# A two-layer decoder trunk on one core: where each engine takes its batches of expert pairs is read from a table, in place of step lengths and a common lag

## The chip, the cores and the metric

The kernel runs on one core of a Trainium2 chip, in one launch. The metric is the device time of that launch in microseconds (us), the median over runs. The core has five engines that run their own instruction streams and meet on semaphores: TensorE (PE in the profile), VectorE (DVE), ScalarE (ACT), GpSimd (POOL) and SyncE (SP), and 16 DMA engines that all of them feed.

## The reference, cut to what matters

```python
for l in range(DEPTH):                       # DEPTH = 2, x is (1, 256, 1024) f32
    h = _rmsnorm(x, norm_mix_g[l])
    z = h @ w_in[l]                          # split into q, k, v, gates, conv and pool inputs
    ...                                      # sparse attention, conv branch, pooling branch
    x = x + jnp.concatenate([o_nsa, o_conv, o_pool], axis=-1) @ w_out[l]
    x = x + _cross_attention(_rmsnorm(x, norm_xa_g[l]), _rmsnorm(mem, norm_mem_g[l]), xa_wq[l], xa_wkv[l], xa_wo[l])
    x = x + _peer(_rmsnorm(x, norm_ffn_g[l]), peer_wq[l], peer_subkeys[l], peer_u[l], peer_v[l])
return _rmsnorm(x, final_g)

def _peer(h, wq, sub_keys, u, v):            # per token: 8 heads x 16 experts = 128 pairs
    ...                                      # top 16 of each key half, top 16 of their 256 sums
    act = jax.nn.gelu(jnp.einsum('cd,chkd->chk', hc, u[ic]))      # ic: 128 expert numbers a token
    return jnp.einsum('chk,chkd->cd', gc * act, v[ic])
```

Each of the 256 tokens picks 128 of 16384 experts in each layer. An expert is one row of `u` and one of `v`, 1024 numbers each, so a token's pair is 8 KB that must be gathered from memory.

## The kernel before

The 256 tokens are two tiles of 128, and with two layers there are four pieces of dense work (everything but the experts' sums) and four of expert work. The program is five stages, written by one function `stage(dense, experts, ...)`. The first stage does the dense work of layer 0, tile 0. Stages 1, 2 and 3 each do the dense work of the next tile and, woven into it, the expert work of the tile before. The last stage has only expert work and what is left of the ranking of its experts. In the profiled execution the stages 1, 2, 3 and last begin at 217.4, 633.5, 1035.8 and 1432.3 us.

**Expert work.** A stage has 128 pairs, `k` = 0 to 127. GpSimd issues one gather a pair (`gather`, L521): 128 rows of 8 KB, one a token, into one of 10 slots of `uv_rows` (`ROWS`). Two pairs are a batch, so a stage has 64 batches (`NB`). For each pair of a batch VectorE forms the dot product of the gathered `u` rows with the tokens (L566), ScalarE takes the gelu and scales a 128x64 diagonal with it (L1029, L1036), and TensorE multiplies the `v` rows with that diagonal and adds them up in PSUM (L1307, four matmuls a pair); its last matmul frees the slot (`slots_free`), and GpSimd may gather the pair that stands 10 further on. The first 10 gathers of the next stage are issued in this manner at the end of a stage, as soon as a quarter of its experts is ranked (`gates0`).

**Dense work.** Its steps stand in a list (`PLAN`; stage 1 has `MEM_PLAN`, with the keys and values of layer 1's memory besides; the last stage `LAST_PLAN`). An engine that has part in a step runs it when the list comes to it; `zk2`, for instance, is a product on TensorE and a copy on ScalarE, `rope` is VectorE alone. The weights are loaded by SyncE in units of 1 MB, each as soon as the unit that held its place has been used; stages 1 and 3 have 7 places, stage 2 has 3 (the two first blocks go to places that stage 3 still uses). The product of four units with a rows' operand is L1361 or L1337.

**The order of the two.** Each engine's program is one sequence. The helper `run` goes through the list, and behind each step it puts as many batches as the table `turns` has for that engine and step:

```python
for step_name in ["start"] + plan:
    if step_name in steps:
        steps[step_name]()
    n = turns.get(name, {}).get(step_name, 0)
    if n:
        batch_run(b, b + n)
        b += n
```

`turns` is worked out by `spread`: each step has a length (`LENGTH`), the batches are dealt out in proportion to the lengths passed, VectorE and ScalarE get the same numbers (ScalarE one batch later at the start), and TensorE stands one batch behind them (`LAG`). Stages 2 and 3 have one table. In the last stage 21 batches are dealt out over the ranking, and the rest follows behind it. The ranking of a quarter of the experts is seven steps on VectorE: `rank`, `rank_more`, `rank_pairs`, `rank_pairs_more`, `gates`, `look_up`, `look_up_more`; of these ScalarE has part in `gates` alone.

Of the kernel before, what the change touches and what calls it, by code (L numbers as in the profile page):

```python
# [41 lines left out]
NB = PAIRS // B  # L42
# [26 lines left out]
for _name, _w in (("causal", S), ("cadd", TILES * NC), ("cvalid", TILES * NC), ("cur", 4 * P), ("prev", 4 * NC),  # L69
# [95 lines left out]
LAST_PLAN = ["rank1", "rank_more1", "rank_pairs1", "rank_pairs_more1", "gates1", "look_up1", "look_up_more1",  # L165
             "rank2", "rank_more2", "rank_pairs2", "rank_pairs_more2", "gates2", "look_up2", "look_up_more2",
             "rank3", "rank_more3", "rank_pairs3", "rank_pairs_more3", "gates3", "look_up3", "look_up_more3",
             "first_out"]


LENGTH = {"mix_norm": 4, "ab": 4, "zq": 4, "zk1": 4, "zk2": 4, "conv_in": 0, "conv": 2, "rope": 3, "branch_gates": 0,
          "sel_exps": 0, "win_exps": 0, "sel_values": 4, "win_values": 4, "turn_kv": 5, "rank": 3, "rank_more": 2, "rank_pairs": 3, "rank_pairs_more": 3, "look_up": 3, "look_up_more": 3,
          "gates": 2, "first_out": 2, "cmp_in": 6, "cmp_hidden": 6,
          "cmp_hidden_turn": 2, "cmp_kv": 2, "cmp_scores": 4, "sel_scores": 4, "sel_more": 3, "cmp_probs": 3, "cmp_out": 3,
          "sel_turn": 4, "win_scores": 4, "win_more": 3, "sel_out": 2, "conv_norm": 4, "win_turn": 4, "conv_act": 3, 
          "win_out": 2, "small_branches": 3, "mix_turn": 2, "wo": 9, "xa_norm": 7, "xq": 8, "xa_scores": 6,
          "xa_turn": 4, "xa_out": 4, "xo": 9, "ffn_norm": 8, "pq": 8, "sub_scores": 2, "mem_kv": 8}
LAG = 1
AT_START = 1


def spread(plan, within):

    lengths = [LENGTH[name if name in LENGTH else name.rstrip("0123456789")] for name in plan]
    vector, tensor, done, passed = {"start": AT_START}, {}, 0, 0
    for name, length in zip(plan, lengths):
        passed += length
        due = within * passed // sum(lengths)
        vector[name] = due - done
        tensor[name] = max(due - LAG, 0) - max(done - LAG, 0)  # L190
        done = due
    scalar = {**vector, "start": 0, plan[0]: vector[plan[0]] + AT_START}
    tensor[plan[0]] += AT_START
    return {"vector": vector, "scalar": scalar, "tensor": tensor}


TURNS = spread(PLAN, NB - 2)
MEM_TURNS = spread(MEM_PLAN, NB - 2)
LAST_TURNS = spread(LAST_PLAN, 21)


TURN_PARTS = [6.25]
# [26 lines left out]
def build_program(nc, a):  # L229
    with ExitStack() as ctx:  # L230
        def sb(name, shape, dt=F32):
            return ctx.enter_context(nc.sbuf_tensor(name, shape, dt))
# [23 lines left out]
        conv = sb("conv", [P, 2, P])  # L256
# [14 lines left out]
        gates = sb("gates", [P, 24])  # L271
# [20 lines left out]
        cmp_in = area2[:, 0:1024].rearrange("p (k c n) -> p k c n", k=2, c=16)  # L292
# [35 lines left out]
        def stage(dense, experts, mem_layer=None, first=False, last=False):  # L328


            plan = LAST_PLAN if last else FIRST_PLAN if first else PLAN if mem_layer is None else MEM_PLAN
            turns = {} if first else LAST_TURNS if last else TURNS if mem_layer is None else MEM_TURNS
            if dense is not None:
                layer, tile = dense // TILES, dense % TILES
            own_half = dense is not None and tile == 0
# [98 lines left out]
            def run(eng, name, steps, batch_run):  # L434

                b = 0
                for step_name in ["start"] + plan:
                    if step_name in steps:
                        steps[step_name]()
                    n = turns.get(name, {}).get(step_name, 0)  # L440
                    if n:
                        batch_run(b, b + n)
                        b += n
                if experts is not None:
                    batch_run(b, NB)


            with nc.Block(no_gpsimd_drain=not last) as block:
# [109 lines left out]
                def _(dve):  # L558
# [420 lines left out]
                    for i in range(4):  # L979
                        steps[f"gates{i}"] = lambda i=i: expert_gates(i)  # L980
                        signal = "routed" if i else "first_routed"
                        for part, more in enumerate(("", "_more")):
# [6 lines left out]
                            if first and i == 0:  # L989
                                steps[f"rank{more}0_later"] = lambda p=part: rank_half(range(2, 4), p)  # L990
                                steps[f"rank_pairs{more}0_later"] = lambda p=part: rank_pairs(range(1, 2), p)
                                steps[f"look_up{more}0_later"] = lambda p=part: look_up(range(1, 2), "first_routed", p)
                    run(dve, "vector", steps, batch_run)
                    if experts is not None:
                        experts_end()
# [14 lines left out]
                def _(act):  # L1010
# [271 lines left out]
                    if first:  # L1282
                        steps["pq0"] = lambda: queries("PQ0", 0, 2)
                        steps["pq0_later"] = lambda: queries("PQL", 2, 2)
                        steps["sub_scores0"] = lambda: sub_scores("PK0", 0, 2)
                        steps["sub_scores0_later"] = lambda: sub_scores("PKL", 2, 2)
                    run(act, "scalar", steps, batch_run)
                    if last:
                        for c in range(2):
# [7 lines left out]
                def _(pe):  # L1297
# [378 lines left out]
                    if first:  # L1676
                        steps["pq0"] = lambda: cols_product("PQ0", "pq0", [0])
                        steps["pq0_later"] = lambda: cols_product("PQL", "pq0", [1])
                        steps["sub_scores0"] = lambda: sub_scores("PK0", 0, 2, 1)
                        steps["sub_scores0_later"] = lambda: sub_scores("PKL", 2, 2, 2)  # L1680
                    run(pe, "tensor", steps, batch_run)


            nc.gpsimd.sem_clear(range(stage_sems[0], stage_sems[-1] + 1))
            nc.all_engine_barrier(sem_only=True)

        stage(0, None, mem_layer=0, first=True)
        stage(1, 0, mem_layer=1)
        for s in range(1, STAGES - 1):
            stage(s + 1, s)  # L1690
# [117 lines left out]
```

## Time and profile before

| | us |
|---|---|
| median of 3 runs | 1760.89 (1759.98 to 1761.31) |
| the profiled execution's own time | 1762.63 |
| its span | 1760.8 |
| PE, DVE, ACT, POOL busy | 1338.8, 1094.5, 515.2, 663.1 |
| moved by DMA | 689.00 MB, of it 536.90 MB by GpSimd's gathers |

The busy times are those of the whole span. GB/s of a stretch is what all DMA engines moved in it, gathers and weights together. A gather is 128 x 8 KB, 1.05 MB.

### The profile page before, as it was taken

The numbers are of one execution on the slowest core, as the hardware profiler recorded it, in microseconds if no ns is written. First come the engines' busy times: TensorE is split into PE (matmuls) and PEld (weight loads), VectorE is DVE, ScalarE is ACT, GpSimd is POOL, SyncE is SP. The second block draws the span as 40 slices with busy tenths as digits, with TensorE's granted clock in tenths as the row PEclk, the third lists the DMA queues.
The fourth block names the chain that finished last, engine by engine and source line by source line (L and its number), as shares of the span: only waits on it lengthen the run. The fifth ranks groups of instructions, "written<-read, shape, count | busy, mean of one in ns | idle before, by whom it ended". The sixth has DMA issues, their size and how long they took to land. (4 is left out here: it accounts for less than half of the span.)

```text
span 1760.8 us, 22766 instructions
## 1 busy us (share of the span) xinstructions
PE 1338.8 (76%) x8310; PEld 686.1 (39%) x8310; DVE 1094.5 (62%) x2746; ACT 515.2 (29%) x1295; POOL 663.1 (38%) x1028
## 2 busy tenths in 40 slices
PE   8999886679999857667888766767888865565655
PEld 5856842245564523222354433233354531111111
DVE  5510588984333849779434757798444868964444
ACT  3411232262312222226332222225332323221112
POOL 0000234344333424435434434344433545565451
PEclk9999988799999978878989888778999977887778
DMA  9755599999999999999999999999999999999996
GB/s 387 293 169 182 209 421 421 414 394 422 411 421 421 420 410 405 421 396 414 422 421 422 421 421 420 422 386 421 421 421 421 421 418 400 407 420 422 421 421 272
DMA packets 95728, 689.00 MB, mean 391 GB/s; under 512 B 11008, under 2 KB 11136, under 8 KB 12288
## 3 DMA queue, kind: packets, MB, share of 16 engines
q0 software_dynamic: 73728, 536.90, 74.0%
q1 hardware_dynamic: 21888, 150.64, 21.3%
q8 instruction: 66, 1.08, 0.2%
q14 instruction: 46, 0.38, 0.1%
HBM read 685.40 MB, written 2.10 MB: 390 GB/s over the span
## 5 line engine op out<-in xcount | busy, mean ns | idle before, releaser
L521 POOL DMA_INDIRECT uv_rows<-uv_in,idx x512 | 504.0, 984 | 1055.5 <-PE acc_pe L1307 817.5
L1307 PE MATMUL acc_pe<-uv_rows,diag 64*64 64x512 f32 x4096 | 616.5, 731 | 322.7 <-ACT diag L1036 307.9
L566 DVE CUSTOM_DVE_ANT_0 uv_rows<-uv_rows,h_ps 128x1024 f32<-128x1024 f32 x512 | 606.7, 1218 | 232.4 <-DMA uv_rows<-uv_in,idx 220.6
L1307 PEld LDWEIGHTS acc_pe<-uv_rows,diag 64*64 64x64 f32 x4096 | 154.5, 153 | 693.1 <-ACT diag L1036 481.8
L1029 ACT ACTIVATE gelu_b<-act_b,h_scale 128x2 f32<-128x2 f32 x255 | 75.0, 294 | 744.0 <-DVE act_b L566 739.1
L1337 PEld LDWEIGHTS bank<-h_t,w_own 128*128 128x128 f32 x1504 | 171.0, 193 | 18.0 <-issue 18.0
L1361 PE MATMUL bank<-w_own,h_t 128*128 128x512 f32 x384 | 176.0, 612 | 2.3 <-ACTq L1077 2.2
L1337 PE MATMUL bank<-h_t,w_own 128*128 128x128 f32 x1504 | 175.1, 278 | 0.0
L515 POOL TENSOR_TENSOR diag<-ident_st,gate 128x64 f32<-128x64 f32 x512 | 159.0, 311 | 9.6
L1036 ACT ACTIVATE diag<-diag,gelu_b 128x64 f32<-128x64 f32 x510 | 149.6, 340 | 8.3
L1361 PEld LDWEIGHTS bank<-w_own,h_t 128*128 128x128 f32 x384 | 73.2, 196 | 107.8 <-issue 103.7
L828 DVE TENSOR_TENSOR xs<-xs,bank 128x512 f32<-128x512 f32 x16 | 11.0, 688 | 160.1 <-PE bank L1361 160.1
L1074 ACT ACTIVATE area<-bank 128x512 f32<-128x512 f32 (+2 forms) x77 | 43.2, 561 | 226.4 <-PE bank L1337 130.0
L680 DVE SCALAR_TENSOR_TENSOR conv<-hc,smalls,conv 128x128 f32<-128x128 f32 x240 | 68.3, 355 | 0.4
L1332 PE MATMUL bank<-ident,area 128*128 128x128 f32 x216 | 36.0, 319 | 30.6 <-ACT area L1049 20.6
L1029 ACT ACT_TABLE_LOAD x40 | 51.3, 1283 | 1.8
L1332 PEld LDWEIGHTS bank<-ident,area 128*128 128x128 f32 x216 | 28.7, 163 | 50.8 <-issue 23.1
L566 DVE DVE_READ_ACCUMULATOR2_ANT act_b<- 128x1 f32 x512 | 42.1, 82 | 0.0
L864 DVE MAX8 half_v<-area 128x8 f32<-128x128 f32 x128 | 28.0, 279 | 19.2 <-ACTq L1077 18.9
L598 DVE TENSOR_TENSOR h_t<-bank,smalls 128x512 f32<-128x512 f32 x24 | 15.7, 688 | 36.6 <-PE bank L1332 27.7
L867 DVE FIND_INDEX8 half_i<-half_v,area 128x8 uint32<-128x128 f32 x128 | 34.2, 285 | 0.0
L1337 PE MATMUL bank<-h_t,uv_rows 128*128 128x128 f32 x288 | 32.9, 275 | 1.0 <-DVE h_t L598 1.0
(208 smaller groups left out, 1170.5 us busy)
## 6 DMA issues: line engine op xcount, KB each, us to landing
w_own<-blocks_in SPq DMA_DIRECT2D x112, 1024.0 KB, 10.5
uv_rows<-blocks_in SPq DMA_DIRECT2D x24, 1024.0 KB, 10.4
uv_rows<-uv_in,idx POOLq DMA_INDIRECT x512, 15.4
xs<-x_in SPq DMA_DIRECT2D x2, 512.0 KB, 13.5
uv_rows<-mem_in SPq DMA_DIRECT2D x1, 1024.0 KB, 13.8
mem_gained<-uv_rows SPq DMA_DIRECT2D x1, 1024.0 KB, 14.1
area<-mem_gained SPq DMA_DIRECT2D x1, 1024.0 KB, 8.9
smalls<-smalls_in SPq DMA_DIRECT2D x1, 816.5 KB, 13.5
```

The lines of the kernel that those rows point to most:

```text
L515: nc.gpsimd.tensor_tensor(diag[:, slot_of(k, earlier), :], ident_st[:, :], gate[:, k:k + 1].to_broadcast([P, HT]), ALU.mult).then_inc(sems ...
L521: nc.gpsimd.indirect_dma_start(uv_rows[:, slot_of(k, earlier), :, :].rearrange("p a n -> p (a n)"), None, a["uv"], bass.IndirectOffsetOnAx ...
L566: v.tensor_tensor_reduce(u_row, u_row, h_ps[:, :], 1.0, 0.0, ALU.mult, ALU.add, act_b[:, k // B % AHEAD, k % B:k % B + 1]).then_inc(sems[" ...
L680: ins = v.scalar_tensor_tensor(out=conv[:, g, :], in0=hc[:, g, k:k + P], scalar=small("cw", g * CONV_W + k, 1), in1=conv[:, g, :], op0=ALU ...
L867: step.mark(v.max_index(where[:, g, lo], top[:, g, lo], values(g)))
L1029: s.activation(gelu_b[:, b % AHEAD, :], act_b[:, b % AHEAD, :], ACT.Gelu_apprx_tanh, scale=h_scale[:, 0:1]).then_inc(sems["gelu_done"], 1)
L1036: s.activation(diag[:, slot_of(k), :], diag[:, slot_of(k), :], ACT.Copy, scale=gelu_b[:, b % AHEAD, k % B:k % B + 1]).then_inc(sems["diag_ ...
L1074: drain(s.activation(out, src, func, **kw), job)
L1307: mm = pe.matmul(acc_pe[c * HT:(c + 1) * HT, r * BLK:(r + 1) * BLK], diag[tok, slot_of(k), :], uv_rows[tok, slot_of(k), 1, c * BLK:(c + 1) ...
L1332: mm = pe.transpose(out[:, i * P:(i + 1) * P], src, ident[:, :])
L1337: mm = pe.matmul(out, lhs, rhs, start=(i == 0), stop=(i == len(pairs) - 1))
L1361: mm = pe.matmul(out[:, :], lhs[:, c, :], w[:, i, :], start=(c == 0), stop=(c == KC - 1))
```

## The change

`LENGTH`, `LAG`, `AT_START` and `spread` go, and with them the three tables that it made. In their place stands a table that is written out: for each of the stages 1, 2, 3 and last (`None`), for each step, how many batches VectorE, ScalarE and TensorE run behind it. The steps, their order on each engine, the order of the batches, the gathers' and weights' order and all waits stay as they were; in the last stage and the others every batch now stands in the table (64 a stage).

```diff
-LENGTH = {"mix_norm": 4, "ab": 4, "zq": 4, "zk1": 4, "zk2": 4, "conv_in": 0, "conv": 2, "rope": 3, "branch_gates": 0,
...
-          "xa_turn": 4, "xa_out": 4, "xo": 9, "ffn_norm": 8, "pq": 8, "sub_scores": 2, "mem_kv": 8}
-LAG = 1
-AT_START = 1
-
-
-def spread(plan, within):
-
-    lengths = [LENGTH[name if name in LENGTH else name.rstrip("0123456789")] for name in plan]
-    vector, tensor, done, passed = {"start": AT_START}, {}, 0, 0
-    for name, length in zip(plan, lengths):
-        passed += length
-        due = within * passed // sum(lengths)
-        vector[name] = due - done
-        tensor[name] = max(due - LAG, 0) - max(done - LAG, 0)
-        done = due
-    scalar = {**vector, "start": 0, plan[0]: vector[plan[0]] + AT_START}
-    tensor[plan[0]] += AT_START
-    return {"vector": vector, "scalar": scalar, "tensor": tensor}
-
-
-TURNS = spread(PLAN, NB - 2)
-MEM_TURNS = spread(MEM_PLAN, NB - 2)
-LAST_TURNS = spread(LAST_PLAN, 21)
+BATCHES = {
...
+        "xa_turn": (0, 1, 1), "xa_out": (2, 2, 2), "xo0": (3, 1, 0), "ffn_norm": (2, 3, 3), "pq0": (1, 1, 2),
...
+    None: {
...
+        "first_out": (38, 41, 40),
+    },
+}
+ENGINES = ("vector", "scalar", "tensor")
...
-            turns = {} if first else LAST_TURNS if last else TURNS if mem_layer is None else MEM_TURNS
+            batches = {} if first else BATCHES[dense]
...
-                    n = turns.get(name, {}).get(step_name, 0)
+                    n = batches[step_name][ENGINES.index(name)] if step_name in batches else 0
```

What this does to the sequences is shown at three places. One line's number in the new kernel is 39 higher than the same line's in the old one.

**TensorE at the start of stage 2.** The rows run from the transposes of the normed tokens through the product `zq` (the first L1361) and `ab` (L1337) to `zk1`. Eight matmuls of `acc_pe` are one batch. Before:

```order
L1332 MATMUL bank<-ident,area 128x128 x8
L1307 MATMUL acc_pe<-uv_rows,diag 64x512 x8
L1361 MATMUL bank<-w_own,h_t 128x512 x8
L1307 MATMUL acc_pe<-uv_rows,diag 64x512 x8
L1337 MATMUL bank<-h_t,w_own 128x128 x32
L1307 MATMUL acc_pe<-uv_rows,diag 64x512 x24
L1361 MATMUL bank<-w_own,h_t 128x512 x8
```

And with the change:

```order
L1371 MATMUL bank<-ident,area 128x128 x8
L1400 MATMUL bank<-w_own,h_t 128x512 x8
L1346 MATMUL acc_pe<-uv_rows,diag 64x512 x32
L1376 MATMUL bank<-h_t,w_own 128x128 x32
L1346 MATMUL acc_pe<-uv_rows,diag 64x512 x16
L1400 MATMUL bank<-w_own,h_t 128x512 x8
```

The batch ahead of `zq` is gone from there, and four stand between `zq` and `ab` where one stood.

**TensorE in stage 3, from `zq` to the transposes of q, k and v.** The three L1361 of before are `zq`, `zk1` and `zk2`. Before:

```order
L1361 MATMUL bank<-w_own,h_t 128x512 x8
L1307 MATMUL acc_pe<-uv_rows,diag 64x512 x8
L1337 MATMUL bank<-h_t,w_own 128x128 x32
L1307 MATMUL acc_pe<-uv_rows,diag 64x512 x24
L1361 MATMUL bank<-w_own,h_t 128x512 x8
L1307 MATMUL acc_pe<-uv_rows,diag 64x512 x40
L1361 MATMUL bank<-w_own,h_t 128x512 x8
L1307 MATMUL acc_pe<-uv_rows,diag 64x512 x16
L1332 MATMUL bank<-ident,area 128x128 x8
```

And with the change:

```order
L1400 MATMUL bank<-w_own,h_t 128x512 x8
L1376 MATMUL bank<-h_t,w_own 128x128 x32
L1346 MATMUL acc_pe<-uv_rows,diag 64x512 x24
L1400 MATMUL bank<-w_own,h_t 128x512 x8
L1346 MATMUL acc_pe<-uv_rows,diag 64x512 x40
L1400 MATMUL bank<-w_own,h_t 128x512 x8
L1346 MATMUL acc_pe<-uv_rows,diag 64x512 x8
L1371 MATMUL bank<-ident,area 128x128 x8
```

With the batch ahead of `zq`, which is gone too, 8 batches now stand ahead of `zk2` where 10 stood, and 9 ahead of the transposes where 12 stood. On VectorE `rope` stands between the two: behind 10 batches where it stood behind 11.

**VectorE in the last stage, from the end of the first ranked quarter.** L936 ends `look_up_more1`; MAX, MAX_INDEX and MATCH_REPLACE are `rank2`, the next MAX and MAX_INDEX `rank_more2`; a pair is two rows of L566, a batch four. Before:

```order
L936 TENSOR_TENSOR idx<-area 128x32
L566 ISA uv_rows,act_b<-uv_rows,h_ps 128x1024
L566 ISA act_b 128x1
L566 ISA uv_rows,act_b<-uv_rows,h_ps 128x1024
L566 ISA act_b 128x1
L864 MAX half_v<-area 128x8 x4
L867 MAX_INDEX half_i<-half_v,area 128x8 x4
L871 MATCH_REPLACE area<-half_v,area 128x128 x4
L566 ISA uv_rows,act_b<-uv_rows,h_ps 128x1024
L566 ISA act_b 128x1
```

And with the change:

```order
L975 TENSOR_TENSOR idx<-area 128x32
L903 MAX half_v<-area 128x8 x4
L906 MAX_INDEX half_i<-half_v,area 128x8 x4
L910 MATCH_REPLACE area<-half_v,area 128x128 x4
L903 MAX half_v<-area 128x8 x4
L906 MAX_INDEX half_i<-half_v,area 128x8 x4
L605 ISA uv_rows,act_b<-uv_rows,h_ps 128x1024
L605 ISA act_b 128x1
L605 ISA uv_rows,act_b<-uv_rows,h_ps 128x1024
L605 ISA act_b 128x1
```

The batches behind `look_up_more1` and behind `rank2` are moved to later places. Over the stage, the batches that stand behind VectorE's steps are these (steps from `start`; a dot where there is none): before, one behind `start` and one behind each of the 22 steps but for `rank_more1`; now none behind `start`, then 1 1 . 1 1 2 . for the first quarter, . 1 3 . 1 . 1 for the second, 2 . 2 1 2 6 1 for the third, and the last 38 behind `first_out`.

**Elsewhere, in numbers of batches ahead of a step.** TensorE comes to `zk2` behind 6, 8 and 8 batches in stages 1, 2 and 3, where it had 8, 10 and 10; in stage 1 to `sel_values0` behind 21, where it had 23; in stage 2 to `xo0` behind 43, where it had 45, and then runs none behind `xo0` and `xo1`, where it ran two behind each, and three behind the transposes of `ffn_norm`. In stage 3 it runs 44 ahead of `xa_out` and no more until behind those transposes. VectorE comes to `xo0` in stage 2 behind 44 batches, where it had 46; in both kernels TensorE runs 17 batches ahead of the compression product of stage 2.

## Rows read from the trace of the kernel before

**Rows 1.** the page, part 2: GB/s in 40 slices of 44 us

```profile
GB/s 387 293 169 182 209 421 421 414 394 422 411 421 421 420 410 405 421 396 414 422 421 422 421 421 420 422 386 421 421 421 421 421 418 400 407 420 422 421 421 272
```

**Rows 2.** busy time by stretch; last columns granted clock, DMA share, GB/s

```profile
core 0: us, PE busy (x) PEld busy (x) DVE busy (x) ACT busy (x) POOL busy (x), PEclk, DMA share, GB/s
217.00:320.00 103.00, 71.95 (x396) 32.00 (x400) 89.74 (x286) 28.63 (x66) 37.09 (x56) 0.82 1.01 421
320.00:400.00 80.00, 61.41 (x487) 31.04 (x487) 72.82 (x166) 42.78 (x108) 35.95 (x56) 0.89 1.00 403
...
610.00:690.00 80.00, 59.20 (x396) 32.47 (x388) 52.83 (x159) 22.40 (x51) 32.11 (x51) 0.87 1.00 406
...
740.00:780.00 40.00, 22.53 (x175) 7.81 (x179) 29.55 (x75) 6.16 (x21) 13.39 (x20) 0.70 0.99 391
...
1130.00:1170.00 40.00, 26.70 (x224) 10.46 (x223) 36.40 (x95) 13.34 (x37) 17.35 (x27) 0.74 0.97 382
...
1430.00:1550.00 120.00, 64.81 (x356) 16.23 (x360) 103.26 (x293) 31.72 (x80) 56.75 (x86) 0.76 1.00 407
1550.00:1740.00 190.00, 112.97 (x644) 27.16 (x640) 96.76 (x160) 35.28 (x120) 96.89 (x152) 0.77 1.01 421
```

**Rows 3.** who waited for whom over the whole span: total, times, longest

```profile
POOL uv_rows L521 <- PE acc_pe L1307: 817.5, 276, 18.8
...
DVE uv_rows L566 <- DMA uv_rows<-uv_in,idx: 220.6, 144, 3.8
...
DVE area L697 <- ACTq L1077: 18.2, 3, 8.0
```

**Rows 4.** timeline of stage 3: start, length, engine, line; idle time before it

```profile
1110.34 8.12 PE L1361 MATMUL bank<-w_own,h_t 128*128 128x512 f32 x16
...
1118.57 0.60 ACT L1074 ACTIVATE area<-bank 128x512 f32<-128x512 f32 x1 [6.39 <-PE bank L1361]
...
1119.24 0.27 DVE L697 TENSOR_TENSOR area<-area,cos_t 128x112 f32<-128x112 f32 x1 [8.02 <-ACTq L1077]
```

**Rows 5.** gathers' issue at the start of stage 2

```profile
662.03 0.97 POOL L521 DMA_INDIRECT uv_rows<-uv_in,idx  x1 [8.22 <-PE acc_pe L1307]
...
671.71 0.98 POOL L521 DMA_INDIRECT uv_rows<-uv_in,idx  x1 [6.93 <-PE acc_pe L1307]
```

**Rows 6.** busy time by stretch, right behind the issue of 671.71

```profile
672.00:680.00 8.00, 8.00 (x44) 3.12 (x37) 6.94 (x19) 4.06 (x7) 7.12 (x11) 1.00 0.94 320
```

**Rows 7.** PE at the compression step of stage 2

```profile
754.78 2.80 PE L1471 MATMUL bank<-w_own,area 128*32 128x256 f32 x48 [0.82 <-DVE area L723]
765.24 1.94 PE L1471 MATMUL bank<-w_own,area 128*32 128x256 f32 x16 [7.67 <-DMA w_own<-blocks_in]
```

**Rows 8.** GpSimd at the compression step of stage 2

```profile
769.40 0.97 POOL L521 DMA_INDIRECT uv_rows<-uv_in,idx  x1 [13.82 <-PE acc_pe L1307]
```

**Rows 9.** the chain that ended last, start of the last stage and 21st batch

```profile
1434.38 1.22 DVE uv_rows L566
...
1439.92 1.22 DVE uv_rows L566
...
1444.29 0.69 DVE area L903
...
1447.75 1.22 DVE uv_rows L566
...
1451.94 1.13 DVE uv_rows L566
...
1457.36 1.13 DVE uv_rows L566
...
1462.16 1.22 DVE uv_rows L566
...
1467.87 1.13 DVE uv_rows L566
...
1539.20 1.21 DVE uv_rows L566
```

More of the change, by code:

```diff
@@ L168 @@
              "first_out"]
-LENGTH = {"mix_norm": 4, "ab": 4, "zq": 4, "zk1": 4, "zk2": 4, "conv_in": 0, "conv": 2, "rope": 3, "branch_gates": 0,
[L172 to L176, printed above, removed]
-          "xa_turn": 4, "xa_out": 4, "xo": 9, "ffn_norm": 8, "pq": 8, "sub_scores": 2, "mem_kv": 8}
@@ L197 @@
-TURNS = spread(PLAN, NB - 2)
-MEM_TURNS = spread(MEM_PLAN, NB - 2)
-LAST_TURNS = spread(LAST_PLAN, 21)
+BATCHES = {
[7 rows of a table added]
+        "sel_scores": (1, 0, 0), "sel_exps": (0, 0, 1), "cmp_probs": (0, 0, 1), "conv4": (1, 1, 0),
+        "conv5": (0, 0, 1), "cmp_out": (1, 0, 0), "win_scores": (0, 2, 0), "win_more": (1, 0, 0),
+        "win_exps": (0, 2, 0), "conv6": (1, 0, 0), "conv7": (0, 0, 1), "sel_values0": (1, 1, 2),
+        "sel_values1": (0, 1, 0), "sel_out": (1, 0, 1), "conv_norm": (0, 0, 1), "win_turn": (1, 0, 0),
+        "conv_act": (1, 1, 1), "win_values1": (0, 0, 1), "win_out": (2, 1, 0), "small_branches": (0, 2, 0),
+        "mix_turn": (0, 0, 2), "wo0": (2, 2, 0), "wo1": (0, 0, 1), "xa_norm": (1, 1, 0), "xq0": (4, 3, 3),
+        "xq1": (0, 0, 1), "xa_scores": (1, 1, 1), "xa_turn": (3, 2, 2), "xa_out": (0, 1, 1), "xo0": (0, 3, 0),
[4 rows of a table added]
+    },
[7 rows of a table added]
+        "cmp_hidden_turn": (1, 0, 0), "cmp_kv": (0, 0, 1), "conv2": (0, 0, 1), "cmp_scores": (0, 1, 0),
+        "sel_scores": (1, 1, 3), "sel_exps": (1, 1, 0), "cmp_probs": (2, 0, 0), "conv4": (1, 0, 0),
+        "conv5": (0, 1, 1), "cmp_out": (0, 1, 1), "sel_turn": (0, 1, 0), "win_scores": (1, 0, 0),
+        "win_more": (1, 0, 0), "win_exps": (1, 0, 0), "conv7": (0, 1, 1), "sel_values0": (2, 2, 2),
+        "sel_values1": (0, 1, 1), "sel_out": (2, 3, 1), "conv_norm": (0, 0, 1), "win_turn": (2, 1, 0),
+        "conv_act": (1, 0, 1), "win_out": (0, 0, 1), "small_branches": (0, 1, 1), "mix_turn": (3, 4, 1),
+        "wo1": (1, 0, 4), "xa_norm": (0, 1, 0), "xq0": (2, 0, 0), "xq1": (0, 2, 2), "xa_scores": (1, 1, 0),
+        "xa_turn": (0, 1, 1), "xa_out": (2, 2, 2), "xo0": (3, 1, 0), "ffn_norm": (2, 3, 3), "pq0": (1, 1, 2),
[3 rows of a table added]
+    },
[8 rows of a table added]
+        "cmp_kv": (1, 0, 1), "conv2": (0, 0, 1), "conv3": (1, 2, 0), "cmp_scores": (0, 0, 1), "sel_scores": (2, 0, 1),
+        "sel_exps": (0, 1, 0), "cmp_probs": (0, 1, 0), "conv4": (0, 1, 0), "cmp_out": (3, 1, 1),
+        "sel_turn": (1, 0, 1), "win_scores": (0, 1, 0), "win_exps": (0, 1, 1), "conv6": (0, 1, 0), "conv7": (0, 0, 1),
[3 rows of a table added]
+        "xq1": (2, 1, 0), "xa_turn": (2, 2, 3), "xa_out": (2, 1, 0), "xo1": (1, 2, 0), "ffn_norm": (0, 2, 3),
[3 rows of a table added]
+    },
[6 rows of a table added]
+        "first_out": (38, 41, 40),
+    },
+}
```

40 rows, old and new, of the table BATCHES are left out of this document.

## Prediction

> **What bounds the kernel now.** I read the GB/s line first, since an engine's busy share over the span says little about a kernel that moves 689 MB. From the sixth slice on nearly every slice stands at 420 to 422 GB/s [rows 1], although no engine is full there: the DMA engines are the bound, and 421 GB/s is their rate. The first 200 us are slower, but the change does not touch that stage. The waits say the same: GpSimd waits 817.5 us in all for TensorE to free a slot, and VectorE 220.6 us for gathers to land [rows 3]. Neither is a fault, since a full queue looks like this from both ends.
>
> So the bytes set the time, and the order of the batches can only give or take time in which the DMA engines had too little in their queue. How much is that? I cut the span into stretches where the rate holds and where it sags. Against 421 (217 to 320 us and 1550 to 1740 us), the sagging stretches lose (421 - rate) / 421 of their length [rows 2]:
>
> - 320 to 400 us (stage 1): 403, 3.4 us
> - 610 to 690 us (end of stage 1, start of stage 2): 406, 2.85 us
> - 740 to 780 us (stage 2): 391, 2.85 us
> - 1130 to 1170 us (stage 3): 382, 3.7 us
> - 1430 to 1550 us (last stage): 407, 4.0 us
>
> Together 16.8 us, about 1% of the time. That is the most that this change can win. Behind 1740 us there is only the tail of the last batches, in an order that stays.
>
> The rate is a gather's price: 1.05 MB at 421 GB/s is 2.49 us, so a batch is worth 4.98 us of DMA time, and 10 slots are at most 25 us of cover.
>
> **The change part by part.** No instruction is added or removed; batches move against steps. A freed slot refills the queue, so what counts is when TensorE frees a batch, and whether VectorE gets through its dense steps early enough. I take the five stretches in turn.
>
> *Start of stage 2.* Now TensorE runs one batch, the product `zq`, another, `ab`, then three. GpSimd could issue two gathers at 662.03 us and the next at 671.71 [rows 5], and from 672 to 680 us, before the late ones can deliver, the rate is 320 GB/s [rows 6], 1.9 us lost in 8. In the new order `zq` runs first and four batches follow it. They wait for nothing but VectorE, which does two of them ahead of `rank1` and two right behind `rank_more1`. The four should be free by about 665 us where two were: two batches more, 10 us of queue. I take 2.5 us back; between 0 and 2.85.
>
> *Stage 3, 1130 to 1170 us.* Here VectorE is the slow one: 36.4 of 40 us busy [rows 2]. Just ahead of it VectorE stands still for 8.02 us at `rope`, until ScalarE has copied the product `zk2`, which ran from 1110.34 for 8.12 us on TensorE [rows 4]. TensorE could not start it earlier, because 10 batches stood ahead of it, the tenth of which VectorE finishes only just before. With the change 8 stand there; VectorE has still `look_up2`, `look_up_more2` and two batches to do, by the last stage's rows 2.4 + 3.3 + 2 x 2.37 = 10.4 us [rows 9], which covers 8.12 us. What is left is the wait for ScalarE, which does the same two batches before its copy, some 1.6 us. VectorE wins 6.4 us, time for 2.7 batches, or 13 us of DMA. That is more than the 3.7 us lost: I take 3.7, between 0 and 3.7. The price is that TensorE frees its first batch only behind `ab`, two products of some 8 us later. The cover is the unlanded part of the 10 gathers issued at the stage's end and the units that `zq` and `ab` set free; it should just do.
>
> The same wait is in stages 1 and 2; all three are 18.2 us [rows 3], so 10.2 us for these two. The new tables put `zk2` behind 6 and 8 batches there where 8 and 10 stood.
>
> *Stage 2, 740 to 780 us.* Beside VectorE's lag there is a wait of its own: with three places the fourth unit of the compression weights is loaded only when the first is used, TensorE stands 7.67 us for it [rows 7], and GpSimd gets no slot for 13.82 us [rows 8]. Before and after, 17 batches stand ahead of that product, so the wait stays. VectorE's part goes. I take 2.0 us; between 0 and 2.85.
>
> *Stage 1, 320 to 400 us.* VectorE is 72.8 of 80 us busy [rows 2]. It gains by its shorter wait at `rope`, but TensorE now comes to `sel_values0` with 21 batches done, not 23, and so frees two of them later. I take 2.4 us; between 0 and 3.4.
>
> *Last stage.* Here the change should cost. VectorE has no pause between 1434 and 1541 us but at `gates`, and the rate is what it leaves. From the starts of its dots [rows 9] a batch takes 2.37 us and the steps, as distances less a batch: `rank` 3.2, `rank_more` and `rank_pairs` together 5.5, `rank_pairs_more` 1.8, `gates` 3.05 (it waits for ScalarE), `look_up` 2.4, `look_up_more` 3.3, 19.3 us a quarter. A batch is late by its end minus 4.98 us for each batch before it, and the queue's loss is the greatest lateness less a constant. Before, the 21st batch ends at 1539.20 + 2.37, 107.2 us behind the first dot: late by 107.2 - 20 x 4.98 = 7.6 us. The loss measured is 4.0, so the constant is 3.6. With the change the 15th batch comes behind two quarters (the second's `gates` waits less, 18.4 us), 8.6 us of the third and 15 batches: 46.3 + 35.5 = 81.8 us, late by 81.8 - 14 x 4.98 = 12.1. The 8th, behind 28 us of steps, is late by 46.9 - 34.9 = 12.0. Loss 12.1 - 3.6 = 8.5 us, 4.5 more than now. The six batches behind `look_up3` come too late to mend it. The end of stage 3 may shift what has landed by then, by a gather or so: 2 to 6 us.
>
> *New dry spells.* In stage 2 TensorE now has no batch from `xo0` through `xo1` to the transposes of `ffn_norm`, two products of 8.12 us and some 7 us, 23 us. Four units (10 us) and up to 8 gathers are in the queue. At 6 gathers it is 25 us, and nothing is lost. Stage 3 has a like stretch with more units. I take 0.6 us; between 0 and 8.
>
> **Sum.** 2.5 + 3.7 + 2.0 + 2.4 = 10.6 us back, 4.5 + 0.6 = 5.1 us lost, 5.5 us net. From the profiled execution's 1762.63 us (its span is 1760.8, with 1.8 around it) that is 1757.1; the median of the runs is 1.74 lower, 1760.89, so 1755.4.
>
> **The rivals.** *All of it comes back, also in the last stage.* If fewer gathers have landed when the last stage begins, VectorE's lateness has more cover: three gathers fewer are 7.5 us, more than the 4.5 lost there. With the other stretches at their bounds (12.8 us) the time is about 1748. For it: the new tables differ for stages 2 and 3, where one served both. Against it: stage 3's end looks as late as before.
>
> *The gaps only move.* A queue that is refilled earlier in one place is emptier in the next, and the bytes are the same: 1761. For it: 1550 to 1740 us and 217 to 320 us show that a full queue stays full whatever the engines do [rows 2], and the places where TensorE stands behind in the new tables lie right behind those where it gained. The Trainium skill, in "DMA: Bandwidth & Descriptors", section "Issuing engines are not separate DMA queues", says that transfers issued by SyncE and GpSimd run on the same 16 engines and interleave. By that alone, weights loaded earlier take their time from gathers, and only an empty queue is worth anything; the sum would be 0 where the queue still holds a unit or a gather in the sagging stretches. The rows of this case put a price on a thin queue all the same: 320 GB/s at a DMA share of 0.94 [rows 6].
>
> *Slower: TensorE's stretch without a batch in stages 2 and 3.* If only two gathers are unlanded when `xo0` begins, cover is 5 + 10 us against 23: 8 us dry in stage 2, some 6 in stage 3 behind its `xa_turn`. With the last stage's 4.5 and 10.6 us back, 8 us net lost: 1769. It decides as soon as fewer than four gathers are in flight there. VectorE has done 44 batches and TensorE 43, which bounds them between 0 and 8.
>
> **How the numbers follow.** The forecast, 2 to 9 us faster, 0.45; all comes back, 0.16; gaps only move, within 3 us, 0.23; slower, 0.16. Half of a slower or a better case lies beyond 1766 and 1746, so the range 1745 to 1766 leaves some 0.2 out; it also holds the bounds of each term taken singly. The likeliest case's own range is 1752 to 1759. A measurement tells 0.2%, 3.5 us, from no change. Faster by more than that takes most of the first case (0.40) and the second: 0.56. Within it: the rest of the first, and the third: 0.28. Slower: 0.16.
>
> **What would show it.** Right: 421 GB/s from 672 to 680 us and through stage 3's compression step; a wait at `rope` below 3 us in each of three stages; the last stage's first 120 us below 400 GB/s, with a loss near 8.5 us. Wrong: a last stage at 407 or better, sags in the places where TensorE's batches were taken out (`xo0`, `xo1`, `wo0`, `wo1`), or the wait at `rope` unchanged.

## The result, and the profile after

The new tables make the kernel slower: median 1787.5 us (1779.7 to 1787.8, 4 runs) against 1761.1 us (1760.0 to 1764.1) in the same session, a ratio of 1.0136 (95% interval 1.0106 to 1.0167). The profiled execution took 1787.51 us, with a span of 1785.7 against 1760.8. The prediction was 1755.4, range 1745 to 1766. Two executions further down were far slower than the others of their kernel (1819.01 us of e4_new1's ten, 3182.55 us of m3_wo_xo's four): the medians count them, the ratios leave them out.

Where do the 24.9 us of span lie? The stages begin with the transposes of L1684 (L1645 before). In the profile after:

```profile
634.49 0.87 PE L1684 MATMUL h_ps<-ident,h_t 128*128 128x128 f32 x3 [4.73 <-PEq L1724]
1048.07 1.35 PE L1684 MATMUL h_ps<-ident,h_t 128*128 128x128 f32 x7 [3.20 <-PEq L1724]
1452.35 0.87 PE L1684 MATMUL h_ps<-ident,h_t 128*128 128x128 f32 x3 [4.29 <-PEq L1724]
```

Stage 1 starts at 217.2 us, where it started at 217.4. By these starts stage 1 is 1.1 us longer (417.3 for 416.1), stage 2 is 11.3 longer (413.6 for 402.3), stage 3 7.8 (404.3 for 396.5), the last 4.9 (333.4 for 328.5). The page's line of GB/s, in slices of 44.6 us, shows where stages 2 and 3 lose most, slice 18 (341) and slice 28 (346):

```profile
GB/s 387 301 166 179 223 420 421 402 394 418 406 421 421 420 421 420 422 341 420 402 401 384 421 421 405 421 421 346 412 421 400 421 420 359 422 422 421 422 421 269
```

Cut into stretches, as [rows 2] were (the last column is GB/s):

```profile
310.00:410.00 100.00, 78.38 (x528) 38.65 (x529) 82.13 (x193) 43.68 (x113) 42.93 (x66) 0.86 0.99 399
620.00:700.00 80.00, 53.86 (x328) 27.99 (x327) 56.57 (x174) 20.65 (x46) 28.13 (x43) 0.81 1.01 421
750.00:790.00 40.00, 24.33 (x180) 11.53 (x180) 28.24 (x73) 12.62 (x34) 10.59 (x16) 0.68 0.86 333
860.00:960.00 100.00, 83.70 (x560) 49.87 (x558) 37.94 (x68) 27.35 (x63) 35.57 (x56) 0.98 0.98 389
1060.00:1090.00 30.00, 30.00 (x152) 16.30 (x156) 28.07 (x87) 6.99 (x15) 8.01 (x12) 0.91 0.99 397
1130.00:1180.00 50.00, 30.52 (x219) 10.28 (x222) 44.59 (x114) 17.54 (x45) 22.64 (x36) 0.81 1.01 421
1200.00:1230.00 30.00, 16.09 (x105) 7.39 (x107) 26.25 (x56) 14.75 (x41) 8.36 (x13) 0.77 0.85 336
1350.00:1370.00 20.00, 16.51 (x107) 9.55 (x106) 9.05 (x16) 5.68 (x11) 7.65 (x12) 0.91 0.94 372
1452.00:1572.00 120.00, 62.38 (x376) 16.87 (x376) 101.34 (x288) 31.11 (x81) 60.50 (x92) 0.76 0.99 398
1572.00:1750.00 178.00, 97.59 (x572) 23.44 (x576) 91.30 (x152) 33.02 (x110) 89.35 (x140) 0.76 1.01 421
```

Counted as in the prediction, (421 - rate) / 421 of each length, two stretches won: the start of stage 2 (620 to 700 us) loses nothing where 2.85 us were lost, and stage 3 from 1130 to 1180 nothing where 3.7 were. Five lost: 750 to 790 us 8.4 (2.85 before), 860 to 960 us 7.6 (0 before), 1060 to 1090 us 1.7 (0), 1200 to 1230 us 6.1 (0), 1350 to 1370 us 2.3 (0). The last stage's first 120 us lose 6.6 (4.0 before), stage 1 5.2 (3.4). The difference of the nine is 21 of the 24.9 us; the rest is not placed.

Only SyncE (weights) and GpSimd (gathers) issue transfers while the stages run. Each of the five has its mark in GpSimd's issue of gathers, a long wait for TensorE to free a slot:

```profile
773.51 1.08 POOL L560 DMA_INDIRECT uv_rows<-uv_in,idx  x1 [27.87 <-PE acc_pe L1346]
...
942.40 0.97 POOL L560 DMA_INDIRECT uv_rows<-uv_in,idx  x1 [18.85 <-PE acc_pe L1346]
...
1078.28 0.97 POOL L560 DMA_INDIRECT uv_rows<-uv_in,idx  x1 [32.16 <-PE acc_pe L1346]
...
1214.61 0.97 POOL L560 DMA_INDIRECT uv_rows<-uv_in,idx  x1 [15.44 <-PE acc_pe L1346]
...
1359.77 0.98 POOL L560 DMA_INDIRECT uv_rows<-uv_in,idx  x1 [20.77 <-PE acc_pe L1346]
```

The first is the compression step of stage 2, where 13.82 us stood in [rows 8]. Three more long waits stand ahead of the one at 942 us:

```profile
870.99 0.97 POOL L560 DMA_INDIRECT uv_rows<-uv_in,idx  x1 [15.93 <-PE acc_pe L1346]
...
897.61 0.97 POOL L560 DMA_INDIRECT uv_rows<-uv_in,idx  x1 [15.14 <-PE acc_pe L1346]
...
912.58 0.97 POOL L560 DMA_INDIRECT uv_rows<-uv_in,idx  x1 [9.31 <-PE acc_pe L1346]
```

The kernel before had one of 12.88 us in the same place, which cost nothing:

```profile
923.26 0.97 POOL L521 DMA_INDIRECT uv_rows<-uv_in,idx  x1 [12.88 <-PE acc_pe L1307]
```

A long wait need not be dear. The one at the start of stage 2, after the change, stands in a stretch that loses nothing:

```profile
659.40 0.97 POOL L560 DMA_INDIRECT uv_rows<-uv_in,idx  x1 [26.16 <-PE acc_pe L1346]
```

The whole sum of these waits hardly moved, and the longest did (the first row below; 817.5 us and 18.8 in [rows 3]). So a total of waits says nothing here; the longest ones show where to look, but not the price. VectorE's wait at `rope` went as forecast:

```profile
POOL uv_rows L560 <- PE acc_pe L1346: 838.8, 246, 32.2
...
DVE uv_rows L605 <- DMA uv_rows<-uv_in,idx: 314.2, 207, 4.8
...
DVE area L736 <- ACTq L1116: 3.4, 3, 1.5
```

The wait at 1214 us has another engine behind it. In the profile after, TensorE waits 12.16 us for ScalarE's diagonal, and ScalarE stands in the exponentials (L1188) until VectorE has scored the second half of the heads:

```profile
1202.49 0.49 ACT L1188 ACTIVATE area<-area,st 128x256 f32<-128x256 f32 x1
...
1207.88 0.51 ACT L1188 ACTIVATE area<-area,st 128x256 f32<-128x256 f32 x1 [4.79 <-DVE st L793]
...
1212.33 3.61 PE L1346 MATMUL acc_pe<-uv_rows,diag 64*64 64x512 f32 x16 [12.16 <-ACT diag L1075]
```

VectorE's new place for two batches is between `sel_scores` and `sel_more`; ScalarE's for the first of them is behind `sel_exps`, and that step waits for `sel_more`. The dots are there by 1204 us, but the diagonal only at 1212.

### The profile page after: what moved, and what is told of

The parts are those of the page before. It is cut to its first block and busy times, and to the rows that moved or that the text cites. A ratio compares the mean times of both kernels' runs of the same rounds, so it can differ in the third digit from the quotient of the medians.

```text
span 1785.7 us, 22754 instructions
## 1 busy us (share of the span) xinstructions
PE 1326.4 (74%) x8310; PEld 694.8 (39%) x8310; DVE 1099.5 (62%) x2746; ACT 513.5 (29%) x1294; POOL 663.2 (37%) x1028
## 5 line engine op out<-in xcount | busy, mean ns | idle before, releaser
L1346 PE MATMUL acc_pe<-uv_rows,diag 64*64 64x512 f32 x4096 | 594.4, 716 | 299.7 <-ACT diag L1075 292.9
L1346 PEld LDWEIGHTS acc_pe<-uv_rows,diag 64*64 64x64 f32 x4096 | 158.2, 153 | 661.3 <-ACT diag L1075 445.1
L1068 ACT ACT_TABLE_LOAD x39 | 50.0, 1283 | 1.9 <-ACT area L1113 0.4
L903 DVE MAX8 half_v<-area 128x8 f32<-128x128 f32 x128 | 28.0, 279 | 18.8 <-ACTq L1116 16.5
L1510 PE MATMUL bank<-w_own,area 128*32 128x256 f32 x240 | 22.0, 541 | 21.6 <-DVE area L762 15.8
```

The lines of the kernel that those rows point to most:

```text
L1068: s.activation(gelu_b[:, b % AHEAD, :], act_b[:, b % AHEAD, :], ACT.Gelu_apprx_tanh, scale=h_scale[:, 0:1]).then_inc(sems["gelu_done"], 1)
L1346: mm = pe.matmul(acc_pe[c * HT:(c + 1) * HT, r * BLK:(r + 1) * BLK], diag[tok, slot_of(k), :], uv_rows[tok, slot_of(k), 1, c * BLK:(c + 1) ...
```

## The experiments

**One stage at a time.** The earlier rule's numbers, written as a table, replace the new ones in one stage; the fourth kernel has the new table in stage 1 alone.

```diff
+BATCHES[2] = as_table(TURNS)          # e1_old2
...
+BATCHES[3] = as_table(TURNS)          # e2_old3
...
+BATCHES[None] = as_table(LAST_TURNS)  # e3_old_last; e4_new1: all three of these
```

> The changed kernel with the earlier table (lengths and lag) back in stage 2 alone. Theory, each stage loses by itself: stage 2 lasted 402.3 us before (633.5 to 1035.8) and 413.6 after (634.5 to 1048.1), so 11.3 us come back, 1787.5 - 11.3 = 1776, 0.9% slower than before. Rival, the queue's shortage is handed on from stage to stage: stage 3 and the last start from another state and lose more or less; below 5 or above 16 us back would speak for it.

> The changed kernel with the earlier table back in stage 3 alone. Each stage by itself: stage 3 lasted 396.5 us before and 404.3 after, so 7.8 us come back, about 1779.7. Rival, handed on: stage 3's loss is partly what a late stage 2 leaves it (its first gather stands 32 us behind the last one), then less than 4 us come back.

> The changed kernel with the earlier table back in the last stage alone. Each stage by itself: the last stage lasted 328.5 us before and 333.4 after, 4.9 us come back, about 1782.6; the prediction's formula for VectorE's lateness gives 4.5. Rival: the last stage is longer because stage 3 leaves it fewer landed gathers, then less than 2 us come back.

> The changed kernel with the earlier table back in stages 2, 3 and last, so that only stage 1 has the new one. Each stage by itself: stage 1 lasted 416.1 us before and 417.2 after, so about 1762, the same as before within what can be measured. The prediction had 2.4 us and more back in stage 1: 1757. Rival, handed on: the new end of stage 1 (all 64 batches freed a product earlier) empties the queue at the start of stage 2 with the earlier table, 1766 or more.

| kernel | median us | ratio to before (95%) | stages 1, 2, 3, last in its profile, us |
|---|---|---|---|
| changed | 1787.5 | 1.0136 (1.0106 to 1.0167) | 417.3, 413.6, 404.3, 333.4 |
| e1_old2 | 1772.6 | 1.0072 (1.0045 to 1.0098) | 413.7, 400.3, 402.3, 333.6 |
| e2_old3 | 1775.7 | 1.0083 (1.0066 to 1.0100) | 414.6, 414.3, 394.5, 331.6 |
| e3_old_last | 1782.8 | 1.0118 (1.0101 to 1.0135) | 415.6, 414.2, 407.3, 326.8 |
| e4_new1 | 1759.2 | 0.9983 (0.9973 to 0.9994) | 413.1, 402.1, 393.0, 329.2 |

By the ratios, which are taken within one session, 0.64% (11.3 us; 14.9 by the medians) comes back with stage 2, 0.53% (9.3 us; 11.9) with stage 3 and 0.18% (3.2 us; 4.8) with the last stage: together 1.35%, and 1.53% with all three at once. The last stage's 0.18% is not clear of noise by itself, since the two intervals overlap; the lengths are clearer, 326.8 to 329.2 us in the five profiles with the earlier rule of 21 batches and 331.6 to 333.6 in the seven with the new table. Each stage's length goes with its own table whatever the others have, within some 5 us. So the stages lose by themselves, and the rival that the shortage is handed on falls. Stage 1's table is the one part of the change that wins, 0.17% (0.06 to 0.27%); e4_new1 was expected to be no faster than before.

**Inside the stages.** Three edits of the changed kernel's table, each at a place that lost, and all together (m4_all). The numbers are VectorE's, ScalarE's and TensorE's batches behind the step.

```diff
+BATCHES[2]["cmp_in"] = (1, 0, 1)       # m1_cmp; was (1, 0, 0)
+BATCHES[2]["cmp_hidden"] = (0, 0, 1)   # was (0, 0, 0)
+BATCHES[2]["cmp_kv"] = (0, 0, 0)       # was (0, 0, 1)
+BATCHES[2]["conv2"] = (0, 0, 0)        # was (0, 0, 1)
...
+BATCHES[3]["sel_scores"] = (2, 1, 1)   # m2_sel; was (2, 0, 1)
+BATCHES[3]["sel_exps"] = (0, 0, 0)     # was (0, 1, 0)
...
+BATCHES[2]["wo0"] = (0, 0, 2)          # m3_wo_xo; was (0, 0, 0)
+BATCHES[2]["wo1"] = (1, 0, 2)          # was (1, 0, 4)
+BATCHES[2]["xo0"] = (3, 1, 1)          # was (3, 1, 0)
+BATCHES[2]["xo1"] = (0, 0, 1)          # was (0, 0, 0)
+BATCHES[2]["ffn_norm"] = (2, 3, 1)     # was (2, 3, 3)
+BATCHES[3]["xo0"] = (0, 0, 1)          # was (0, 0, 0)
+BATCHES[3]["xo1"] = (1, 2, 1)          # was (1, 2, 0)
+BATCHES[3]["ffn_norm"] = (0, 2, 1)     # was (0, 2, 3)
```

> The changed kernel, with two of TensorE's batches in stage 2 earlier: one behind cmp_in and one behind cmp_hidden, where they stood behind cmp_kv and conv2. Theory, TensorE's stretch without a batch through the compression step dries the queue: GpSimd's wait of 27.9 us there falls to some 15 us (13.8 with the earlier table), and of the 8.4 us that 750 to 790 us lose, some 5 come back: about 1782. Rival, the loss there comes from the unit of compression weights that TensorE waits for (5.8 us), which the edit leaves: no change, 1787.

> The changed kernel, with one of ScalarE's batches in stage 3 ahead of the exponentials (behind sel_scores) where it stood behind them (sel_exps). Theory, ScalarE holds the diagonal of a finished batch back while it waits for VectorE's sel_more: TensorE's wait of 12.2 us at 1212 us falls to some 5 and 4 of the 6.4 us that 1200 to 1230 us lose come back: about 1783. Rival, VectorE's two batches between sel_scores and sel_more are the cause, as they hold the exponentials back: the next batches come no earlier, under 1.5 us back.

> The changed kernel, with one of TensorE's batches behind each of xo0 and xo1 in stages 2 and 3 (they stood behind ffn_norm), and two of the four behind wo1 of stage 2 now behind wo0. Theory, as in the prediction's rival on these stretches: 870 to 880, 910 to 950 and 1360 to 1370 us lose 9.8 us, some 6 come back: about 1781. Rival, the queue is short there because of the weights' order, and batches freed 8 us earlier only move the gap: under 2 us back.

> The three edits together, 14 of the table's entries. If the stretches lose by themselves: 5 + 4 + 6 = 15 us back, about 1772. If the shortage is one and is handed on: less than the best of the three by itself plus 3 us.

| kernel | median us | ratio to before (95%) | stages 1, 2, 3, last in its profile, us |
|---|---|---|---|
| m1_cmp | 1783.9 | 1.0125 (1.0108 to 1.0143) | 414.0, 410.4, 404.2, 332.9 |
| m2_sel | 1781.4 | 1.0104 (1.0087 to 1.0121) | 414.5, 413.0, 403.0, 333.3 |
| m3_wo_xo | 1779.8 | 1.0098 (1.0077 to 1.0119) | 413.5, 408.3, 400.5, 332.9 |
| m4_all | 1770.0 | 1.0043 (1.0028 to 1.0057) | 414.0, 403.6, 398.8, 332.6 |

Back come 0.11%, 0.32% and 0.38% (1.9, 5.6 and 6.7 us; 3.6, 6.1 and 7.7 by the medians), all three together 0.93% (16.4 us; 17.5 by the medians). The interval of each of the three overlaps that of the changed kernel, and only that of m4_all stands clear, so the three single sizes are rough. The stages' lengths help: stage 2 takes 410.4 us with m1_cmp and 408.3 with m3_wo_xo, against 413.0 to 414.3 in the four profiles with its table as it was; stage 3 takes 400.5 with m3_wo_xo, against 402.3 to 407.3, and 403.0 with m2_sel, which lies inside. Together the three add up, so the loss is not handed from one edit's place to another's. Fourteen entries of the table are two thirds of the slowdown.

m1_cmp gave less than the 5 us expected. In its profile GpSimd's wait fell to 13.5 us as it should, but a second one stands behind it, and the stretch still loses (421 - 350) / 421 x 40 = 6.7 us:

```profile
764.19 0.98 POOL L564 DMA_INDIRECT uv_rows<-uv_in,idx  x1 [13.52 <-PE acc_pe L1350]
...
779.62 0.98 POOL L564 DMA_INDIRECT uv_rows<-uv_in,idx  x1 [12.42 <-PE acc_pe L1350]
```

```profile
745.00:785.00 40.00, 25.11 (x180) 11.74 (x180) 29.03 (x78) 12.61 (x35) 9.64 (x15) 0.66 0.86 350
```

One long wait was cut in two. From 750.7 to 779.6 us GpSimd still issues only two gathers, and 28.9 us are worth 11 of them or of the weights' units. The new table is behind in more than one place there: ahead of `sel_scores` it has 19 of TensorE's batches, the earlier one 21. What the rest of the loss hangs on was not taken apart.

m2_sel shows ScalarE's part by itself. In its profile (a line's number is 2 higher than in the changed kernel) the batch comes ahead of the exponentials, TensorE waits 4.83 us in place of 12.16 and GpSimd 7.66 in place of 15.44:

```profile
1203.24 0.30 ACT L1070 ACTIVATE gelu_b<-act_b,h_scale 128x2 f32<-128x2 f32 x1 [7.06 <-DVE act_b L607]
1203.57 0.59 ACT L1077 ACTIVATE diag<-diag,gelu_b 128x64 f32<-128x64 f32 x2
...
1203.97 3.47 PE L1348 MATMUL acc_pe<-uv_rows,diag 64*64 64x512 f32 x16 [4.83 <-ACT diag L1077]
...
1204.18 1.28 ACT L1190 ACT_TABLE_LOAD   x1
...
1206.02 0.98 POOL L562 DMA_INDIRECT uv_rows<-uv_in,idx  x1 [7.66 <-PE acc_pe L1348]
```

The price is two more loads of ScalarE's function table at 1.28 us, gelu's and then the exponential's again. The one shown lies in the time for which ScalarE waited for VectorE before; the other stands ahead of the wait of 7.06 us. In this trace nothing that frees a slot is seen to wait for them. The Trainium skill, in "ScalarE: Activation LUTs", section "What ACT_TABLE_LOAD costs", gives a load about 1283 ns and a switch with its drain some 2.66 us. The trace agrees on the 1.28 us and shows no drain beside it: the load at 1204.18 begins 0.02 us behind the diagonals (1203.57 + 0.59), and the next exponential begins 0.01 us behind the load, at 1205.47.

The wait is gone, but the time that this is worth is not settled. Over 70 us, first the changed kernel and then m2_sel, the loss falls from (421 - 367) / 421 x 70 = 9.0 us to 6.7, as a sag comes back a little later:

```profile
1200.00:1270.00 70.00, 48.79 (x334) 25.33 (x333) 54.82 (x117) 36.53 (x95) 29.89 (x46) 0.83 0.93 367
```

```profile
1200.00:1270.00 70.00, 53.98 (x337) 28.35 (x338) 53.74 (x116) 37.38 (x96) 30.95 (x48) 0.85 0.97 381
```

So the batch cost some 2 us by this profile, which is that of the slowest of four executions (1786.13 us), and 5.6 by the ratio.

m3_wo_xo takes the whole loss of its stretches away; its profile has

```profile
855.00:950.00 95.00, 84.48 (x552) 50.81 (x544) 38.45 (x70) 27.36 (x63) 35.88 (x56) 0.96 1.01 421
1340.00:1360.00 20.00, 18.31 (x117) 10.24 (x110) 9.37 (x18) 5.68 (x11) 7.69 (x12) 1.00 1.01 421
```

where the changed kernel has 389 and 372, with the same products and the same weights in the same order. The rival that the weights' order makes the shortage falls.

**On from the better kernel.** With the new table in stage 1 alone as the base (e4_new1), three terms of the prediction were tried one by one, and together (n4_all).

```diff
-LAST_TURNS = spread(LAST_PLAN, 21)     # n1_last30
+LAST_TURNS = spread(LAST_PLAN, 30)
...
+BATCHES[3]["look_up2"] = (1, 1, 0)     # n2_zk2; was (1, 1, 1)
+BATCHES[3]["look_up_more2"] = (1, 1, 0)  # was (1, 1, 1)
+BATCHES[3]["zk2"] = (0, 0, 2)          # was (0, 0, 0)
...
+BATCHES[2] = joined(WRITTEN, BATCHES[2], PLAN, "look_up_more3")  # n3_start2: the new table up to there
+BATCHES[2]["cmp_in"] = (0, 0, 1)
+BATCHES[2]["cmp_hidden_turn"] = (1, 1, 0)
```

> The kernel with the new table in stage 1 alone (1759.2 us), and in the last stage the earlier rule with 30 batches dealt out over the ranking where it dealt out 21. Theory, VectorE's lateness as the prediction worked it out: a quarter's 19.3 us of steps now stand beside 10 batches, 19.3 + 10 x 2.37 = 43.0 us against 10 x 4.98 = 49.8 us of DMA, the lateness stays below the constant of 3.6 us and the last stage's loss of 3 to 4 us goes: about 1756. Rival, the loss is not VectorE's: the same, 1759; or the ranked experts now come too late for the gathers of the next quarter: 1763 or more.

> The kernel with the new table in stage 1 alone (1759.2 us), and in stage 3 two of TensorE's batches behind zk2 where they stood ahead of it. That is the prediction's term for stage 3 alone: the wait of 8.0 us at rope falls below 3, VectorE has 6 us more, and the stretch behind it (1150 to 1160 us lose 1.6 us in this kernel, 3.7 before) loses nothing: about 1757. Rival, the wait at rope goes but the time is not VectorE's: the same within 1 us.

> The kernel with the new table in stage 1 alone (1759.2 us), and in stage 2 the new table up to look_up_more3, the earlier one behind it, with one batch of TensorE behind cmp_in as in the run m1_cmp. Theory: 660 to 680 us no longer lose their 2.2 us, and the compression step loses no more than with the earlier table: about 1757. Rival, four batches behind zq leave GpSimd 26 us without a free slot, and it shows in a lower rate before or at the compression step: 1760 or more.

> The three edits together on the kernel with the new table in stage 1 alone. If each stretch loses by itself, as the four earlier sums say: 3 + 2 + 2 us back, about 1752, 0.6% faster than before. If the gains were only moved: 1757 or more.

| kernel | median us | ratio to before (95%) | stages 1, 2, 3, last in its profile, us |
|---|---|---|---|
| n1_last30 | 1758.9 | 0.9987 (0.9978 to 0.9996) | 413.8, 402.9, 393.0, 330.5 |
| n2_zk2 | 1758.0 | 0.9974 (0.9963 to 0.9984) | 415.3, 403.0, 391.9, 329.0 |
| n3_start2 | 1757.4 | 0.9974 (0.9964 to 0.9985) | 415.8, 400.0, 396.0, 328.5 |
| n4_all | 1756.8 | 0.9970 (0.9958 to 0.9982) | 414.4, 401.3, 395.2, 326.7 |

All four are faster than the kernel before, n4_all by 5.3 us in its session, yet the intervals of the four and of e4_new1 overlap: of the 7 us expected over e4_new1 some 2 are there. 1752 is missed, and 1756.8 lies at the border of the rival that the gains are only moved (1757 or more), so that this rival is not ruled out here. In their own places the edits did what was expected of them. Behind `rope` in stage 3, first e4_new1, then n2_zk2, where VectorE's wait fell from 6.93 us to 1.51:

```profile
1130.00:1180.00 50.00, 33.70 (x260) 15.47 (x260) 46.26 (x117) 14.14 (x35) 22.81 (x35) 0.76 1.00 407
```

```profile
1130.00:1180.00 50.00, 33.24 (x250) 13.19 (x249) 45.40 (x113) 14.13 (x35) 20.95 (x33) 0.73 1.01 420
```

At the start of stage 2, first e4_new1, then n3_start2, again with a wait of 26.11 us on GpSimd's side; from 740 to 790 us its rate is 420 GB/s, where e4_new1 has 412:

```profile
620.00:700.00 80.00, 53.56 (x316) 25.04 (x312) 59.90 (x181) 20.96 (x49) 31.82 (x49) 0.82 1.00 410
```

```profile
620.00:700.00 80.00, 53.81 (x315) 26.80 (x314) 57.65 (x176) 21.27 (x48) 28.92 (x44) 0.81 1.01 421
```

n1_last30 shows where a gain can go. VectorE's lateness in the last stage, dealt out over 30 batches, is gone. First e4_new1, then n1_last30:

```profile
1425.00:1545.00 120.00, 70.83 (x372) 17.77 (x376) 105.56 (x299) 32.98 (x85) 57.24 (x87) 0.71 1.01 409
```

```profile
1425.00:1545.00 120.00, 70.14 (x392) 17.45 (x392) 100.27 (x283) 27.91 (x80) 61.41 (x96) 0.73 1.01 421
```

That is 3.4 us less lost, and the stage is 1.3 us longer in these two profiles. In them the tail, the time behind the last gathers, gave the gain back. The chain that ended last passes through TensorE there. In e4_new1:

```profile
1715.40 19.99 DMA uv_rows<-uv_in,idx
1737.40 1.95 PE acc_pe L1388 x16
```

and in n1_last30:

```profile
1707.36 18.89 DMA uv_rows<-uv_in,idx
...
1728.27 3.69 PE acc_pe L1388 x16
1731.96 3.88 PE bank L1383 x6
1735.84 1.88 PE acc_pe L1388 x16
```

A batch's eight matmuls are sixteen records here. The fourth batch from the end takes 3.69 us in n1_last30; in e4_new1 that batch takes 1.95, and so does the one shown. TensorE is mostly at the lower of its two levels there, 1.2 GHz (granted clock 0.55 from 1723 to 1733 us in n1_last30; 0.72 and 1.00 in the last 20 us of gathers in e4_new1). Its last three batches and the three matmuls on constants that the kernel runs ahead of each (L1383) then take until 1747. What it did before does not tell the two apart: from 1710 to 1720 us TensorE was busy 5.4 of 10 us in n1_last30 and 5.7 in e4_new1.

That is one profiled execution, and the table is not shown to cause it. The kernel before has such an end in its own profile (3.36 us for the fourth batch from the end), and n4_all, with n1_last30's table in the last stage, ends like e4_new1 and has a last stage of 326.7 us. Why the median of n1_last30's 11 runs (1758.9) shows no gain stays open.

## Why the prediction was wrong, by its own steps

- **What bounds the kernel** held: the bytes set the time, and a rate that sagged is not made up for later. What the stages lost simply added; within a stage a sag can come back a little later, as m1_cmp and m2_sel show.
- **Start of stage 2**, 2.5 back: right. 421 GB/s from 620 to 700 us, 2.85 back, in spite of a wait of 26.16 us on GpSimd's side; n3_start2 shows it once more.
- **`rope` and stage 3 behind it**, 3.7 back: right in its stretch. The three waits are 3.4 us in all, for 18.2 in [rows 3], and 1130 to 1180 us run at 421; n2_zk2 shows it with this one move alone.
- **Stage 1**, 2.4 back: right in size. The profiled execution of the changed kernel does not show it, but stage 1 takes 413.1 to 417.3 us in 13 profiles with this table (mean 414.6), 416.1 in the one profile before, and e4_new1 is 0.17% faster, 3.0 us. That all of this is stage 1's is not shown: in e4_new1's profile stage 3, with the earlier table, is 3.5 us shorter too.
- **Last stage**, 4.5 lost: right in size. 4.9 us by the stage's length, 3.2 (ratios) to 4.8 (medians) by e3_old_last. Its first 120 us are below 400 GB/s, but they lose 6.6 us where 8.5 were forecast, so the rate there shows 2.6 of the 4.5. That VectorE's lateness is behind it, n1_last30 shows: with the steps dealt out over more batches nothing is lost there.
- **Stage 2, 740 to 780 us**, 2.0 back: this step failed, by 7.5 us (5.5 lost). "Before and after, 17 batches stand ahead of that product, so the wait stays" counted what stands ahead of the product, and not when the last of it is freed (GpSimd's wait begins at 769.40 - 13.82 = 755.6 us in [rows 8], and at 773.51 - 27.87 = 745.6 after), nor that the two batches right behind the product were gone. m1_cmp, which puts two back, gives 1.9 us of it (3.4 by stage 2's length); the whole earlier table gives back all that stage 2 lost. A count of batches at a step is not a time.
- **New dry spells**, 0.6, "between 0 and 8": the term that failed by most. 860 to 960 and 1350 to 1370 us lose 9.9 us, and m3_wo_xo gives 6.7 of them back. They are the sags at `wo0` to `xo1` that the prediction named as a sign of being wrong. The working granted the stretch a cover of 25 us: four units (each of the two products frees two) and six gathers. But TensorE stands two to four batches behind the earlier table from `xq1` to `xo0`, and waits of 15.9, 15.1 and 9.3 us precede the one of 18.85. Counted from the DMA packets of the two traces, gathers issued less gathers moved, some 3 were in the queue when that wait began, and some 7 when the wait of 12.88 us began before the change, which lost nothing. Fewer than four is what the rival "slower" asked for. The term took the gathers of a fuller queue than the place has.
- **Not in the sum at all: ScalarE.** The prediction read VectorE's and TensorE's columns and took ScalarE, apart from its copy ahead of `rope` and its part in `gates`, as riding along. With its batch behind `sel_exps`, TensorE waits 12.16 us and 1200 to 1230 us lose 6.1. m2_sel brings the wait to 4.83 us and gives back some 2 us by the rate and 5.6 by the ratio, so the size is open.
- **Stage 3's start** "should just do": it did not quite, 1.7 us, with a wait of 32 us.

The gains were 2.85 + 3.7 against 6.2 forecast for these two places, the losses 28 us against 5.1. The rival "slower" had the right kind of place, at 8 us net and a chance of 0.16; the compression step and ScalarE were in no rival.

## What to carry to other kernels

When one resource is full nearly all the time, an order can win only its few gaps and can lose anywhere: here 17 us were to be won, and five places lost 23. Check a new order by the longest time for which nothing frees a buffer, step by step and on every engine of the chain, the small one in the middle too, and start each check from what the gap before has left in the queue. Change one stage at a time: three of four tables lost, and the fourth won 0.17%.

## What was not expected of the hardware

The same order of instructions can lose several us in one execution and nothing in another. Stage 1 with the new table reads 399 GB/s from 310 to 410 us in the changed kernel's profile (above) and, with the same instructions up to there, 421 in e4_new1's; the 13 profiles with this table lie between:

```profile
310.00:410.00 100.00, 79.32 (x550) 38.92 (x543) 83.70 (x194) 45.39 (x117) 41.74 (x65) 0.90 1.01 421
```

Five us, for the same order. What sets it was not tried. A single profile of such a stretch is therefore no measure of an edit worth less than that.
